# Gathering the tokens of routed experts with high and low parts of the rows, with four tables moved to other memory

## The reference, cut to what matters

```python
def moe_swiglu(x, w_router, b_router, w_gate, w_up, w_down):
    logits = (xt @ w_router).astype(jnp.float32) + b_router.astype(jnp.float32)
    top_v, top_i = lax.top_k(logits, TOP_K)
    gates = jax.nn.softmax(top_v, axis=-1)
    ...
    for e in range(N_EXPERTS):
        out = out + combine[:, e:e + 1].astype(xt.dtype) * swiglu(xt, w_gate[e], w_up[e], w_down[e])
```

## Time and profile before

| what | us |
|---|---|
| median of three runs | 1433.57 |
| lowest and highest of them | 1431.04, 1435.57 |
| the profiled execution, whole | 1429.53 |
| its span, first to last instruction | 1427.5 |
| PE busy | 1331.2 (93%) |
| DVE busy | 467.2 (33%) |
| ACT busy | 279.5 (20%) |
| start of the first gather, start of the first expert product | 524.47, 530.96 |
| last piece of the chain in which a down transfer is waited for: start, length | 1382.47, 26.79 |

### The profile page before, as it was taken

One profiled execution on the slowest core, in us unless ns is written; L12 is line 12 of the kernel. 1 busy time (PEld: TensorE's weight loads), 2 busy tenths in 40 slices (PEclk: granted clock), 3 DMA queues, 4 the chain that ended last, 5 costly groups with the idle time before them and its releaser, 6 DMA issues.

```text
span 1427.5 us, 18655 instructions
## 1 busy us (share of the span) xinstructions
PE 1331.2 (93%) x7760; PEld 752.4 (53%) x7760; DVE 467.2 (33%) x1045; ACT 279.5 (20%) x519; POOL 98.8 (7%) x115
## 2 busy tenths in 40 slices
PE   6989899999899969999999999999999999987775
PEld 5846599999675545444544444453433344332322
DVE  7998865554688540031101010110110100100002
ACT  3542443442363100000011010110100101000001
POOL 4530000000550000000000000000000000000000
PEclk9999999999999989999999999999999999999999
DMA  9533344548031197799999969989999999999994
GB/s 283 165 119 118 118 177 177 182 141 296 16 125 60 52 373 255 296 418 409 410 418 409 377 242 377 374 340 410 411 415 411 410 414 412 411 415 411 411 415 193
DMA packets 126734, 423.50 MB, mean 297 GB/s; under 512 B 21632, under 2 KB 23864, under 8 KB 118456
## 3 DMA queue, kind: packets, MB, share of 16 engines
q1 hardware_dynamic: 121464, 421.75, 75.6%
q10 hardware_dynamic: 5184, 0.52, 0.4%
HBM read 421.20 MB, written 1.05 MB: 296 GB/s over the span
## 4 chain that ended last, share of the span: by engine, by line
PE 74%; DMA 14%; DVE 8%; issue 1%; SPq 1%; ACT 1%; POOL 0%; DVEq 0%; ACTq 0%
PE psall L2318 14%; DMA m_ring<-in_moe_w_down_dram 12%; PE psall L2409 11%; PE psall L2332 8%; PE psall L2347 6%; PE psall L2032 4%; PE psall L2420 3%; PE psall L2249 3%; PE psall L2251 3%; PE psall L2130 3%; PE psall L2250 3%; PE psall L2295 2%; PE psall L2196 2%; PE psall L2382 2%; PE psall L2448 2%; PE psall L2231 1%
## 5 line engine op out<-in xcount | busy, mean ns | idle before, releaser
L2332 PE MATMUL psall<-m_ring,xeT 128*64 128x448 f32 x1024 | 204.2, 547 | 23.1 <-DMA m_ring<-in_moe_w_up_dram 23.1
L2409 PE MATMUL psall<-m_ring,hidT 128*64 128x512 f32 (+1 forms) x672 | 201.0, 597 | 15.6 <-DMA m_ring<-in_moe_w_down_dram 14.8
L2318 PE MATMUL psall<-m_ring,xeT 128*128 128x448 f32 x512 | 195.7, 543 | 0.8 <-DVE xeT L1897 0.8
L2332 PEld LDWEIGHTS psall<-m_ring,xeT 128*64 128x64 f32 x1024 | 73.8, 137 | 141.2 <-issue 140.0
L2318 PEld LDWEIGHTS psall<-m_ring,xeT 128*128 128x128 f32 x512 | 97.3, 191 | 94.1 <-issue 92.9
L2409 PEld LDWEIGHTS psall<-m_ring,hidT 128*64 128x64 f32 (+1 forms) x672 | 72.7, 154 | 134.9 <-issue 119.2
L1919 DVE TENSOR_TENSOR hid<-e_silu,psall 64x448 f32<-64x448 f32 x32 | 19.9, 623 | 354.9 <-ACT e_silu L1266 352.9
L1615 DVE TENSOR_TENSOR w_lo<-ring,w_hi 128x1024 fp32r<-128x1024 f32 x66 | 80.4, 1224 | 67.8 <-ACT w_hi L1210 67.6
L2347 PE MATMUL psall<-m_ring,xeT 128*32 128x448 f32 x1024 | 102.0, 542 | 0.0
L2249 PE MATMUL psall<-hnT_hi,w_hi 128*128 128x256 f32 x352 | 99.7, 283 | 0.7 <-DVE hnT_lo L1755 0.7
L2251 PE MATMUL psall<-hnT_hi,w_lo 128*128 128x256 f32 x352 | 99.5, 283 | 0.0
(11 more groups left out here) (327 smaller groups left out, 1455.8 us busy)
## 6 DMA issues: line engine op xcount, KB each, us to landing
m_ring<-in_moe_w_gate_dram SPq DMA_DIRECT2D x128, 896.0 KB, 20.1
m_ring<-in_moe_w_up_dram SPq DMA_DIRECT2D x128, 896.0 KB, 17.1
m_ring<-in_moe_w_down_dram SPq DMA_DIRECT2D x64, 1792.0 KB, 19.0
ring<-in_w_in_dram SPq DMA_DIRECT2D x10, 2048.0 KB, 13.1
ring<-in_ffn_w_gate_dram SPq DMA_DIRECT2D x5, 2048.0 KB, 10.6
ring<-in_ffn_w_up_dram SPq DMA_DIRECT2D x5, 2048.0 KB, 7.8
ring<-in_ffn_w_down_dram SPq DMA_DIRECT2D x5, 2048.0 KB, 8.0
ring<-in_w_out_dram SPq DMA_DIRECT2D x4, 2048.0 KB, 7.9
```

The costliest lines, as they stand in the source:

```text
L2318: ins = M(m_bank(key)[:, 0:MH], x[:, i, 0:P], weights(kind, i, s), start=(i == 0), stop=(i == KT - 1))
L2332: ins = M(m_bank(key)[64 * n:64 * n + 64, 0:MH], x[:, i, 0:64], weights(kind, i, s), start=(i == 0), stop=(i == KT - 1))
L2409: ins = M(y, hidT[:, r, 0:shape[0]], rows(r, 512 * n, 512), **ends)
```

## The change

The rows `hn` of layer 1's feed-forward are split: ACT copies each half of the tokens into `hn_hi` in the short format, ahead of its own work on `hnT`; DVE then writes `hn_lo`, which is `hn` less `hn_hi`, over `hn` itself, behind PE's transposes and its own work on `hnT`. `gather` multiplies both parts by `pick`, which is now of the short format too, and sums them in PSUM: 32 instructions a place where there were 16. It waits for `hn_lo` once.

To make room for `hn_hi`, four tables move: `pick` to the place of `b_raw`, `pickg` to that of `c_raw`, `pickT` to the last third of `cT` (whose old contents are read for the last time ahead of the router), and `logitsT` into `hid`. Their sizes stay.

```diff
+        b_raw_at = nc.sbuf_base - 4 * 2 * PAIRS * GP
...
-        pick = moe("pick", [NT, TMAX + 64])
-        pickg = moe("pickg", [NT, 2 * P])
-        pickT = moe("pickT", [2, NT, P])
+        pick = nc.alloc_sbuf_tensor_at("pick", [P, NT, TMAX + 64], F32R, offset=b_raw_at)
+        pickg = c_raw[:, :, :, :].rearrange("p a b c -> p (a b c)").rearrange("p (t n) -> p t n", t=NT)
+        pickT = cT[:, 2, :, :].rearrange("p (a t) n -> p a t n", a=2)
+        hn_hi = nc.alloc_sbuf_tensor_at("hn_hi", [P, NT, DM], F32R, offset=m_at[0])
+        m_at[0] += 4 * NT * DM
+        hn_lo = nc.alloc_sbuf_tensor_at("hn_lo", [P, NT, DM], F32R, offset=hn_at)
...
-        logitsT = moe("logitsT", [SEQ])
+        logitsT = hid[:, 0:SEQ]
...
                 else:
+                    for t in range(NT):
+                        act.wait_ge(hn_ready, (2 * l + 1) * NT + t + 1)
+                        nc.scalar.activation(hn_hi[:, t, :], hn[:, t, :], ACT.Copy).then_inc(rows_high, 1)
                     xT(l, 1)
...
+            for t in range(NT):
+                arrived(dve, ("xT", 1, 1, 3))
+                dve.wait_ge(rows_high, t + 1)
+                V.tensor_tensor(hn_lo[:, t, :], hn[:, t, :], hn_hi[:, t, :].bitcast(F32), ALU.subtract).then_inc(rows_low, 1)
...
                 pe.wait_ge(v_pick, later(it + 1, 1, k))
+                pe.wait_ge(rows_low, NT)
                 m_open(pe, key, k)
                 for i in range(k0, k1):
                     for t in range(NT):
-                        ins = M(m_bank(key)[:, (i - k0) * n:(i - k0 + 1) * n], hn[:, t, i * P:(i + 1) * P],
-                                pick[:, t, first:first + n], start=(t == 0), stop=(t == NT - 1))
+                        for part in (hn_hi, hn_lo):
+                            ins = M(m_bank(key)[:, (i - k0) * n:(i - k0 + 1) * n], part[:, t, i * P:(i + 1) * P],
+                                    pick[:, t, first:first + n], start=(t == 0 and part is hn_hi),
+                                    stop=(t == NT - 1 and part is hn_lo))
                 event(ins)
```

More of the change, by code:

```diff
@@ L621, in trunk_kernel @@
         ye2 = cT[:, :, :, :].rearrange("p a c n -> p (a c n)")[:, 0:DM]
-        pick = moe("pick", [NT, TMAX + 64])
-        pickg = moe("pickg", [NT, 2 * P])
-        pickT = moe("pickT", [2, NT, P])
+        pick = nc.alloc_sbuf_tensor_at("pick", [P, NT, TMAX + 64], F32R, offset=b_raw_at)
+        assert NT * (TMAX + 64) <= 2 * PAIRS * GP and 2 * NT * P <= 2 * CT * NS and 2 * NT * P <= CT * P
+        pickg = c_raw[:, :, :, :].rearrange("p a b c -> p (a b c)").rearrange("p (t n) -> p t n", t=NT)
[3 more added lines that the diff above has]
+        hn_lo = nc.alloc_sbuf_tensor_at("hn_lo", [P, NT, DM], F32R, offset=hn_at)
         gfin = bT[:, :, :, :].rearrange("p a c n -> p (a c n)")
@@ L694, in trunk_kernel @@
         ffn_silu = sem("ffn_silu")
+        rows_high = sem("rows_high")
+        rows_low = sem("rows_low")
         route_in = sem("route_in")
```

## The result

The changed kernel took 1436.16 us in the median of 20 runs (1431.98 to 1444.05), the kernel before 1432.55 us in 20 (1429.15 to 1435.57). The ratio is 1.0033, with a 95% interval from 1.0021 to 1.0044: slower by 4.7 us (3.6 in the medians, 4.5 in the means), where 0.4 us less was forecast. The profiled execution took 1432.7 us, the second shortest of the 20, with a span of 1430.6, 3.1 us more than that of before.

What follows compares the result with a forecast made beforehand. DMA bytes bound the full stretches and the end after 954 us, PE's chain the rest. Place 0's -0.4 us, all else 0, took 1433.57 (profile plus the median's 4.04 us excess) to 1433.2 us; range 1429.0 to 1439.5.

Steps and rivals of the forecast that it cites:

- place 0's term: First gather, at 524.47 us: falls from 5.72 to 5.3 us, a gain of 0.4, counted in full.
- rival A: Place 0's gather streams half, so the clock stays low there and into the expert product: +2.3 to +3.2 us; 15%.
- What bounds the kernel: DMA bytes pace the full stretches; from 954 us bytes set the end, so only PE changes that move 954 count.
- The transfer near 954: Start of the last full DMA stretch: issued at about 953.6 instead of 954.00; forecast wrong if it moves over 2 us.
- places 4 to 7: Gathers from 953.81 us on, behind the last release that counts: 0 us, even if the clock fell at 5 to 7.
- The pace of few columns: New gather records at full clock: weight loads set 110 to 118 ns each, whatever their columns up to 160.
- Rivals B and C: Short-format gathers: B, few columns stream four times each, +6.0 us, 16%; C, weight loads follow faster, -4.6 us, 5%.
- 20 records in 3.83 us, 12 at 112 ns: Place 0's gather: 189 ns a record at the low clock for 3.83 us, then full clock; 5.3 us in all.
- the main sum: All parts of the change added: -0.4 us, with ends -1.4 and +0.2, giving 1433.2 us.
- as large a share as a 64-column gather had, which kept the high clock: Argument against the low clock at place 0: the short format streams 107 of 189 to 218 ns there.
- Place 2: Gather ending at 704.02 us: saves 0.9 us, but PE's wait near 726 grows from 1.74 to 2.6: 0 us.
- Copies, subtractions, `pick`, moved tables: ACT copies have 0.9 us of cover, DVE subtractions 2.7; `pick` at most 0.14 us, moved tables 0: all hidden.

Runs made afterwards that it cites:

- e6: Changed kernel with place 0 gathered twice in a row; the 64 records took 13.93 us, no whole-kernel time given.
- e3: Changed kernel plus unread products on the identity (8, 6 and 5) in PE's idle stretches ahead of the first gather; ratio 0.9971 to the kernel before, gather 3.80 us.
- e5: Changed kernel once more, unchanged, for another profile; that profiled run took 1438.2 us.
- e1: Changed kernel with place 0 gathered as before (32-bit rows) and the subtractions moved behind place 1's tables; ratio 1.0000 to the kernel before.
- e2: Kernel before with place 0 alone gathered from high and low parts, places 1 to 7 as before; ratio 1.0015 to the kernel before.
- e4: Kernel before plus unread products on the identity (8, 6 and 5) in PE's idle stretches ahead of the first gather; 5.3 us faster than the kernel before.
- e9: Changed kernel with an unread 256-column product behind every fourth product of place 0's gather (8 in all), none ahead of it; ratio 1.0032 to the kernel before.

## Why the prediction was wrong

The step that failed is place 0's term: it let the clock rise inside the gather at 528.3 us as before, although the gather now streams half as much. The runs show a clock of 0.50 through the whole gather and three us beyond, and +2.8 us where -0.4 was forecast. The prediction had this mechanism as rival A, with its size, and gave it 15%.

- **What bounds the kernel**: right. The transfer near 954 moved by 3.20 us and the span by 3.1; places 4 to 7 cost nothing although a low clock now follows place 7's gather (1212 above), as rival A said they might.
- **The pace of few columns**: right at the high clock. 2.85 us for 24 records of 160 columns are 119 ns, 3.80 us for 32 of 128 also; 109 ns for 32 columns (3.48 us for 32). Rivals B and C are out.
- **Place 0, the term that failed.** "20 records in 3.83 us, 12 at 112 ns" took two things. The pace at the low clock, taken as 189 ns from a duration's ratio, is 213 ns (e6), within the bounds and near their upper end. By itself this would have made the gain 0.1 us. What decided it was the 3.83 us themselves, which stand for a clock that comes up at 528.3 as before; the main sum gives no reason for it. It came up only under the product: +1.38 and +1.42 us, the +2.3 to +3.2 of rival A. The argument against A, "as large a share as a 64-column gather had, which kept the high clock", compared two different things, a clock that is high and stays and one that is low and has to rise. The same gather kept 1.00 for 3.80 us in e3 and left 0.50 where it was for 14 us in e6.
- **The price of a weight load.** The rows give 109 ns at the high clock and 213 at the low one (e6, e5). The Trainium skill, "TensorE: Matmul & The Clock Gate", section LDWEIGHTS, gives 107 ns for 128 columns, with no term for the clock; at the high clock the rows agree, at the low one they don't. The Trainium skill says in the same page's Part 1, on the clock gate, that the throttled state is the default and that activity releases it. That agrees with the changed kernel, whose clock is 0.50 behind the waits of the router's chain and rises under the product behind the gather; e6 shows besides that 14 us of gather left it at 0.50.
- **Place 2**: what its gather saved went into the wait, as said (2.56 us in e1, for 2.6 forecast; 2.99 in the changed kernel). That the clock would be low behind a longer wait, 1.7 us, was not thought of; e1 shows that in sum it costs nothing.
- **Copies, subtractions, `pick`, moved tables**: right, all hidden.
- **Size**: 3.1 us in the first profile, 4.7 timed. The runs of the new kernel reach to 1444 us, those of the old to 1436. e5 ties 2.8 us of one such run to a long low stretch at place 3, but the new gather there (32 columns once instead of twice) is not needed for long runs, since e2 has them without it, nor is it enough, since e1 has it and none of them. They come with place 0's gather, by a way that stays open; of the run of 1444 us only its mean clock is known, 0.974, which no run here falls below.

## What to carry to other kernels

Halving what TensorE streams is no gain where weight loads set the pace, and it can be a loss where the engine comes out of an idle stretch: price such a change at both clocks, and ask whether the work left still brings the clock up. Products that nobody reads, put into idle stretches ahead of a serial chain of small products, were worth 5.3 us here (e4), more than the change of the products cost or was forecast to gain. And a shorter piece of work ahead of a transfer that is waited for makes the wait longer, which has a price of its own.

## What was not expected of the hardware

- At the low clock weight loads of 128 columns follow each other at 213 ns, twice the 109 ns of the high one, with 128 columns streamed behind each (e6) and with 32 (e5).
- The clock stayed at 0.50 through 14 us of weight loads back to back with 128 columns of the short format streamed for each (e6), rose after 4 us when eight products of 256 columns were added to the 32 (e9), and, high at the start, stayed at 1.00 through the same 32 in 3.80 us (e3).
- Near 726 us PE's waits of 2.33 to 3.47 us were followed by a low stretch in 7 of 7 profiles (1.6 to 1.7 us lost each), its waits of 1.00 to 1.74 us in none of 5.
